# Reordered tail of the last expert, earlier merge tile, scores over two key tiles, and a modulation row split 2/6

## The reference

```python
# first block
h = rms_norm(x, norm1_g); p = h @ w_in
merged = g_a * (gmlp(...) @ w_up_a) + g_b * (s5(...) @ w_up_b)
x = x + merged @ w_out
h2 = rms_norm(x, norm2_g)
# expert choice: 16 experts, each takes its 128 best tokens
gate, idx = lax.top_k(softmax(h2 @ w_router).T, 128)
xs = h2[idx]
y = (silu(xs @ w_gate) * (xs @ w_up)) @ w_down * gate      # 1024 -> 2048 -> 1024
x = rms_norm(x + segment_sum(y, idx), final_g)
# second block
shift, scale, gate = split(silu(c) @ w_mod + b_mod)
h = rms_norm(x, g_pre) * (1 + scale) + shift
q, k, v, g_att, u, g_lru, merge = split(h @ w_in)
y_a = (dilated_attention(q, k, v) * silu(g_att)) @ w_pa     # 3 groups, 4 heads of 128
y_b = (rg_lru(conv(u)) * silu(g_lru)) @ w_pb
out = (sigmoid(merge_a) * y_a + sigmoid(merge_b) * y_b) @ w_o
return x + gate * rms_norm(out, g_post)
```

## Time and profile before

| | |
|---|---|
| Time, median of 3 | 2869.82 us (2868.81 to 2870.44) |
| The profiled execution's own time | 2869.5 us |
| Its span in the profile | 2867.7 us |
| Mean granted TensorE clock | 0.994 of full |
| TensorE busy | 2804.5 us (98%) |
| VectorE, ScalarE, GpSimd busy | 1720.3, 1308.4, 731.2 us |

### The profile page before, as it was taken

How to read it: one execution, slowest core, us unless ns; L and a number is a source line. 1 busy time by engine, 2 the same in 40 slices (tenths; PEclk the granted TensorE clock), 3 DMA queues, 4 the chain that set the end, 5 groups by cost and what they waited for, 6 DMA issues and landing times. The chain is left out here.

```text
span 2867.7 us, 34973 instructions
## 1 busy us (share of the span) xinstructions
PE 2804.5 (98%) x13294; PEld 2302.4 (80%) x13294; DVE 1720.3 (60%) x1879; ACT 1308.4 (46%) x1544; POOL 731.2 (25%) x283
## 2 busy tenths in 40 slices
PE   7999999989999999999999999999999999999999
PEld 6887888568888888888888867889988777778887
DVE  7962114888888888888888874141312514864132
ACT  4231013467777777777777753130302211343021
POOL 0002222002222233333322322313221323333330
PEclk9999999999999999999999999999999999999999
DMA  4021114599999999999999953111111411111131
GB/s 163 23 72 40 37 52 156 227 387 392 382 384 383 382 382 383 382 384 382 381 380 377 385 202 117 45 60 45 60 49 48 141 44 59 44 44 45 52 125 59
DMA packets 127075, 555.98 MB, mean 194 GB/s; under 512 B 14545, under 2 KB 22753, under 8 KB 93825
## 3 DMA queue, kind: packets, MB, share of 16 engines
q1 hardware_dynamic: 116160, 523.91, 48.1%
q0 software_dynamic: 5328, 20.07, 2.5%
q10 hardware_dynamic: 5490, 10.62, 1.0%
HBM read 521.42 MB, written 32.09 MB: 193 GB/s over the span
## 5 line engine op out<-in xcount | busy, mean ns | idle before, releaser
L2564 DVE TENSOR_TENSOR slots_lo<-buffer,slots_hi 128x2048 fp32r<-128x2048 f32 x384 | 851.4, 2285 | 102.4 <-ACT slots_hi L1849 102.4
L1849 ACT ACTIVATE slots_hi<-buffer 128x2048 fp32r<-128x2048 f32 x384 | 708.9, 1950 | 41.2 <-PE bank L1346 26.2
L1011 PE MATMUL bank<-hT_hi,ring_hi 128*128 128x512 f32 x1216 | 483.8, 398 | 9.7 <-POOL ring_lo L913 6.1
L1013 PE MATMUL bank<-hT_hi,ring_lo 128*128 128x512 f32 x1216 | 474.7, 390 | 0.0
L1012 PE MATMUL bank<-hT_lo,ring_hi 128*128 128x512 f32 x1216 | 474.3, 390 | 0.0
L970 POOL DMA_INDIRECT xacc<-buffer x15 | 276.6, 18438 | 616.4 <-ACT buffer L1915 616.4
L910 POOL CAST ring_hi<-buffer 128x1024 fp32r<-128x1024 f32 x101 | 113.1, 1119 | 848.8 <-DMA buffer<-in_wstream 819.4
L913 POOL TENSOR_TENSOR ring_lo<-buffer,ring_hi 128x1024 fp32r<-128x1024 f32 x111 | 285.0, 2571 | 51.0 <-ACT ring_hi L1579 42.9
L1011 PEld LDWEIGHTS bank<-hT_hi,ring_hi 128*128 128x128 f32 x1216 | 228.9, 188 | 61.9 <-DVE hT_lo L2671 7.1
L1013 PEld LDWEIGHTS bank<-hT_hi,ring_lo 128*128 128x128 f32 x1216 | 228.6, 188 | 48.1
L1012 PEld LDWEIGHTS bank<-hT_lo,ring_hi 128*128 128x128 f32 x1216 | 229.1, 188 | 46.0 <-issue 1.2
(11 more groups left out here) (503 smaller groups left out, 3972.3 us busy)
## 6 DMA issues: line engine op xcount, KB each, us to landing
buffer<-in_w_gate SPq DMA_DIRECT2D x128, 1024.0 KB, 7.7
buffer<-in_w_up SPq DMA_DIRECT2D x128, 1024.0 KB, 4.9
buffer<-in_w_down SPq DMA_DIRECT2D x128, 1024.0 KB, 8.2
buffer<-in_wstream SPq DMA_DIRECT2D x154, 512.0 KB, 3.5
buffer<-in_x SPq DMA_DIRECT2D x16, 512.0 KB, 7.9
od<-buffer ACTq DMA_DIRECT2D x24, 260.0 KB, 2.1
xacc<-buffer SPq DMA_DIRECT2D x8, 512.0 KB, 2.8
h2d<-buffer SPq DMA_DIRECT2D x8, 512.0 KB, 5.0
```

The lines of the kernel that those rows point to most:

```text
L1011: mm(bank, lhs[0], rhs[0], start=first, stop=False)
L1013: return mm(bank, lhs[1], rhs[0], start=False, stop=last)
L1849: fn(slots_hi[:, n_ % NH, :], slots[n_ % NS], ACT.Copy).then_inc(slot_high_ready, 1)
L2564: tt2(slots_lo[:, place_of(n_), :], slots[n_ % NS], slots_hi[:, n_ % NH, :].bitcast(F32), ALU.subtract).then_inc(slot_split, 1)
```

## The change

The text is changed in seven places:

1. Modulation row 3 has 2 of its 8 steps ahead of the index transposes instead of 4, and 6 behind them.
2. The subtraction for the first expert's slot 0 (`slots_lo`, 128x2048) goes from DVE, where it stood between the first expert's index list and the other 15, to POOL, behind the gather; DVE waits for it before it makes the next two.
3. In every expert's down projection PE takes a slot's two steps of f for half 0, then both for half 1. For the last expert a semaphore is given after half 0's last pass, and ACT takes half 0 on it.
4. `last_rows` goes (0,0), (1,0), (0,1), (1,1) in (tile, half), and PE no longer waits for both halves of `last_lo` ahead of it. DVE adds in that order.
5. Scores of a tile with two key blocks: two heads a bank over 256 keys instead of four heads a bank over 128 keys. Masks lie side by side.
6. SP issues the load of tile `I_A2` ahead of its wait for attention's stores and of the loads of the combination.
7. ACT writes `att_hi` of tiles 6 and 7 ahead of the drains of `GA` 2's halves instead of behind both.

The diff, cut to its core:

```diff
     LRU_TILES += [("lg", 2 * _q - 2 + _c) for _c in range(2) if _q > 0]
+LAST_ORDER = [(0, 0), (1, 0), (0, 1), (1, 1)] + [(tt, h) for tt in range(2, 8) for h in range(2)]
...
     for j in range(8):
-        b.add(("last", j // 2, j % 2), "dve")
+        b.add(("last",) + LAST_ORDER[j], "dve")
     for j in range(2):
...
         M0 = 42 * K
-        mask_cur = at(M0, P)
-        mask_prev = at(M0 + 128, P)
+        mask_both = at(M0, 2 * P)
+        mask_prev, mask_cur = mask_both[:, 0:P], mask_both[:, P:2 * P]
         mask_pair = at(M0 + 256, P)
...
                 sp.dma_start(xfd[tt * P:(tt + 1) * P, :], xf3[:, tt, :]).then_inc(xf_stored, 16)
-            for i in range(I_ATT + 4, I_A2):
+            for i in range(I_ATT + 4, I_A2 + 1):
                 load_tile(i)
...
                     comb_loaded[tt], 16)
-            for i in range(I_A2, I_LRU + 4):
+            for i in range(I_A2 + 1, I_LRU + 4):
                 load_tile(i)
...
             gather()
+            pool.wait_ge(slot_high_ready, 1)
+            nc.gpsimd.tensor_tensor(slots_lo[:, place_of(0), :], slots[0], slots_hi[:, 0, :].bitcast(F32),
+                                    ALU.subtract).then_inc(slot_split, 1)
             pool.sem_inc(ys_settled, 1)
...
                 mm(bank[:], ones16[0:NE, :], tables[0:NE, 4 * i:4 * i + 4, :], start=True, stop=True).then_inc(full1, 1)
-            mod_row(3, 0, 4)
+            mod_row(3, 0, 2)
             for j in range(2):
...
                 turn(bank[:, 0:NE], (gv if j else gif)[0][0:NE, :], ident[0:NE, 0:NE]).then_inc(full1, 1)
-            mod_row(3, 4, KD)
+            mod_row(3, 2, KD)
             pe.wait_ge(xs_loaded, 16)
...
                     w = slot_ready(16 + q)
-                    for s in range(2):
+                    if q % 2 == 0:
+                        pe.wait_ge(heT_ready, e * 4 + q // 2 + 1)
+                    for h, s in ((0, 0), (0, 1), (1, 0), (1, 1)):
                         f = 2 * q + s
-                        if f % 4 == 0:
-                            pe.wait_ge(heT_ready, e * 4 + f // 4 + 1)
-                        for h in range(2):
-                            cs = slice(s * DM + h * HALF, s * DM + (h + 1) * HALF)
-                            last = three_passes(psum[6 + h][:], (heT_hi[:, f, :], heT_lo[:, f, :]),
-                                                (w[0][:, cs], w[1][:, cs]), f == 0, f == 15)
+                        cs = slice(s * DM + h * HALF, s * DM + (h + 1) * HALF)
+                        last = three_passes(psum[6 + h][:], (heT_hi[:, f, :], heT_lo[:, f, :]),
+                                            (w[0][:, cs], w[1][:, cs]), f == 0, f == 15)
+                        if not another and (q, h, s) == (7, 0, 1):
+                            last.then_inc(up_full, 1)
                     last.then_inc(slot_used, 1)
...
-                for tt in range(first, end):
-                    for h in range(2):
-                        bank = b2.wait_free(pe, ("last", tt, h))
-                        pe.wait_ge(last_split, h + 1)
-                        hs = slice(h * HALF, (h + 1) * HALF)
-                        mm(bank[:], chosen15[:, tt * P:(tt + 1) * P], last_hi[:, hs], start=True, stop=False)
-                        mm(bank[:], chosen15[:, tt * P:(tt + 1) * P], last_lo[:, hs], start=False,
-                           stop=True).then_inc(full2, 1)
-            pe.wait_ge(last_split, 2)
+                for tt, h in LAST_ORDER[2 * first:2 * end]:
+                    bank = b2.wait_free(pe, ("last", tt, h))
+                    pe.wait_ge(last_split, h + 1)
+                    hs = slice(h * HALF, (h + 1) * HALF)
+                    mm(bank[:], chosen15[:, tt * P:(tt + 1) * P], last_hi[:, hs], start=True, stop=False)
+                    mm(bank[:], chosen15[:, tt * P:(tt + 1) * P], last_lo[:, hs], start=False,
+                       stop=True).then_inc(full2, 1)
             last_rows(0, 4)
...
                 def scores(tt):
-                    for w_ in range(1 + has_previous(g, tt)):
-                        bank = b2.wait_free(pe, ("S", g, tt, w_))
-                        for h in range(HEADS):
-                            last = mm(bank[:, h * P:(h + 1) * P], Qh[:, h, tt * P:(tt + 1) * P],
-                                      Kh[g][:, h, (tt - w_) * P:(tt - w_ + 1) * P], start=True, stop=True)
+                    nw = 1 + has_previous(g, tt)
+                    for w_ in range(nw):
+                        bank = b2.wait_free(pe, ("S", g, tt, w_))[:].rearrange("p (h k) -> p h k", k=nw * P)
+                        for i, h in enumerate(range(HEADS // nw * w_, HEADS // nw * (w_ + 1))):
+                            last = mm(bank[:, i, :], Qh[:, h, tt * P:(tt + 1) * P],
+                                      Kh[g][:, h, (tt - nw + 1) * P:(tt + 1) * P], start=True, stop=True)
                         last.then_inc(full2, 1)
...
                         for h in range(HEADS):
-                            last = turn(bank[:, h * P:(h + 1) * P], SM[tt % 2][:, h, w_ * P:(w_ + 1) * P], ident)
+                            last = turn(bank[:, h * P:(h + 1) * P], SM[tt % 2][:, h, (nw - 1 - w_) * P:(nw - w_) * P], ident)
                         last.then_inc(full2, 1)
...
                     nc.scalar.copy(scB, silu_c.unsqueeze(2).to_broadcast([P, KD, P])).then_inc(scB_ready, 1)
-                    act.wait_ge(slot_used, e * 24 + 24)
+                    act.wait_ge(up_full, e * 3 + 4)
                     for h in range(2):
+                        if h:
+                            act.wait_ge(slot_used, e * 24 + 24)
                         fn(last_hi[:, h * HALF:(h + 1) * HALF], psum[6 + h][:], ACT.Identity,
...
             for i, (kind, x, h) in enumerate(GATT_ORDER):
+                if kind == "GA" and x == 2:
+                    attention_high(6 + h)
                 if i == 1:
...
                         attention_high(x - 2)
-            attention_high(6)
-            attention_high(7)
             for f in (3, 4, 5):
...
-            slots_low(0, 0, 1)
             for e in range(1, NE):
...
             turned_rows_low(first_banks, 1, 2).then_inc(drained1["dve"], 1)
+            dve.wait_ge(slot_split, 1)
             slots_low(0, 1, AHEAD)
...
+            def add_half(tt, h):
+                hs = slice(h * HALF, (h + 1) * HALF)
+                bank = b2.wait_full(dve, ("last", tt, h))
+                dve.wait_ge(x_moved[tt], 64)
+                tt2(xin3[:, tt, hs], bank[:], xin3[:, tt, hs], ALU.add).then_inc(drained2["dve"], 1)
             def add_last(tt):
...
-                for h in range(2):
-                    hs = slice(h * HALF, (h + 1) * HALF)
-                    bank = b2.wait_full(dve, ("last", tt, h))
-                    dve.wait_ge(x_moved[tt], 64)
-                    tt2(xin3[:, tt, hs], bank[:], xin3[:, tt, hs], ALU.add).then_inc(drained2["dve"], 1)
+                for h in range(2 if tt > 1 else 0):
+                    add_half(tt, h)
+                if tt == 0:
+                    add_half(0, 0)
+                    add_half(1, 0)
+                if tt < 2:
+                    add_half(tt, 1)
                 b2.wait_drained(dve, ("last", tt, 1))
...
                         bank = b2.wait_full(dve, ("S", g, tt, w_))
-                        mask = mask_prev if w_ else (mask_pair if g == 2 else mask_cur)
-                        stt(SM[tt % 2][:, :, w_ * P:(w_ + 1) * P], bank[:].rearrange("p (h k) -> p h k", h=HEADS),
-                            HEAD_DIM ** -0.5, mask.unsqueeze(1).to_broadcast([P, HEADS, P]), ALU.mult,
-                            ALU.add).then_inc(drained2["dve"], 1)
+                        mask = mask_both if nw == 2 else (mask_pair if g == 2 else mask_cur)
+                        heads = HEADS // nw
+                        stt(SM[tt % 2][:, heads * w_:heads * (w_ + 1), 0:nw * P],
+                            bank[:].rearrange("p (h k) -> p h k", h=heads), HEAD_DIM ** -0.5,
+                            mask.unsqueeze(1).to_broadcast([P, heads, nw * P]), ALU.mult, ALU.add).then_inc(drained2["dve"], 1)
                     b2.wait_drained(dve, ("S", g, tt, nw - 1))
```

## The result

Five executions of the changed kernel have a median of 2855.85 us (2852.97 to 2857.6), five of the kernel before, on the same chip, 2870.44. The ratio is 0.9946, 95% interval 0.9935 to 0.9956: faster, by 14.6 us. The profiled execution took 2853.83 us, its span 2851.7 (2867.7 before), and its mean granted clock is 0.997 against 0.994. Predicted were 2854.8, with a range of 2851.5 to 2859.5.

A forecast was written before the change was run, and what follows sets the result against it. PE, busy 2804.5 us (98% of the span), was taken as the bound, leaving pauses and slow clocks to win; 6.6 + 4.3 + 3.0 + 0.4 + 0.4 = 14.7 us off 2869.5 gave 2854.8, range 2851.5 to 2859.5.

The forecast's parts named there:

- 1, `GA` 6's early load: Merge's first tile: loading it early removes PE's pause (5.08) and the slow passes behind it (1.54), 6.6 us.
- 2, `att_hi` 6 and 7: Before products A: roundings done in ACT's idle time remove the pause (2.74) and slow passes (1.61), 4.3 us.
- 3, the last expert's tail: Behind the last expert: working by halves brings the gate row 3.3 us nearer, 3.0 us net, ends 2.3 and 3.3.
- 4, in front of the first expert: Before the first expert: row steps moved at no cost, subtraction off DVE's queue; 0.4 us, ends 0 and 2.4.
- 5, scores: Attention scores of eleven two-key-block tiles: fewer, wider products win 0.4 us, ends 0 and 0.8.
- the allowance for the chain of adds, squares and norms: Last expert's tail: 0.3 us taken off the 3.3 because this chain might be late next.
- the term's own end of 2.4: Before the first expert: upper end of the 0.4 us gain, if the shorter pause kept the clock up.
- still 1.95 us before the gathered rows land at 582.27: Before the first expert: modulation row 3, ending 1.8 us later at 580.3, still finishes ahead of the gathered rows.
- 0.45 earlier: First expert: DVE's second half of xsT_lo could end at 586.5 instead of 586.96.
- the prediction's better rival: Before the first expert: the clock stays up, 2.0 us more won, 2852.8; chance 0.08.
- the gate row's price: Scores: 0.429 us per 512 columns, by which 8 records of 256 take 1.72 us, 0.07 less.
- The rivals that end slower or near no change: Merge's early load not coming early, 2861.4, chance 0.03; all experts' passes slower in the new order, 2875, chance 0.02.

The follow-up runs named there:

- e5: Kernel before, only the load of tile GA6 moved ahead of the attention rows; 2865.26 us, ratio 0.9979.
- e6: Kernel before, only the last two att_hi roundings moved ahead of the last two gate fills; 2867.36 us, ratio 0.9987.
- e7: Kernel before, only the down projection by halves and the last expert's rows in the new order; 2868.83 us, ratio 0.9992.
- e2: Kernel before, only the first slot's subtraction moved to GpSimd behind the gather; 2869.25 us, ratio 1.0001.
- e3: Kernel before, modulation row by 2 and 6 and first slot's subtraction on GpSimd, nothing else; 2869.14 us, ratio 0.9994.
- e8: Kernel before, only the scores over two key tiles at once; 2872.6 us, ratio 1.0005.
- e4: Kernel after, with the first slot's subtraction back on VectorE ahead of the gather; 2855.95 us, ratio 0.9948.
- e9: Kernel before, first slot's subtraction on VectorE behind the gathered rows' low parts, nothing on GpSimd; 2870.23 us, ratio 0.9997.
- e11: Kernel after, first passes wait for only half the low parts, modulation's last two VectorE operations moved into the last expert; 2851.95 us, ratio 0.9933.
- e12: Kernel after with the changes of e10 and e11 together; 2854.09 us, ratio 0.9938.
- e1: Kernel before, only the modulation row by 2 and 6 instead of 4 and 4; 2869.7 us, ratio 0.9995.
- e10: Kernel after, final norm's first two tiles reordered: four adds before the first multiplication, squares before weighted ones; 2854.73 us, ratio 0.9944.

## Why the prediction held, step by step

| term (its number in the prediction) | forecast | trace after | alone |
|---|---|---|---|
| 1, `GA` 6's early load | 6.6 | 6.63 | 6.62 (e5) |
| 2, `att_hi` 6 and 7 | 4.3 | 4.35 | 4.33 (e6) |
| 3, the last expert's tail | 3.0 | 2.46 | 2.39 (e7) |
| 4, in front of the first expert | 0.4 | 2.66 | to the first pass 1.83 (e2), 0.53 with the row slow (e3) |
| 5, scores | 0.4 | 0.66 | 0.61 (e8) |

**1 and 2** were right in mechanism and size. The pauses went whole, and the slow passes behind them with them. `GA` 7 came in time. From the attention's last transposes to the first `OT` the kernels without edit 6 take 30.58 to 32.48 us, as the pause (4.10 to 5.38) and the slow stretch behind it turn out; with it 24.57 or 24.58 in all six. The gain is 6.0 to 7.9 us, and a steadier stretch.

**3** was right at the gate row, 3.25 us nearer where 3.3 was forecast. The size that failed is the allowance for the chain of adds, squares and norms, 0.3; it came to 0.8. The chain did start earlier, but its multiplication L2669 stood against GpSimd's subtraction. In seven kernels (after, e3, e4, e7, e9, e11, e12) the first multiplication starts 0.17 to 1.97 us into a GpSimd subtraction, and in each it ends 1.08 us behind that subtraction's end, whatever its start: after, 1686.47 + 2.39 = 1688.86 and 1687.17 + 2.77 = 1689.94. In the four that have edits 3 and 4 and the old order of squares, the pause before the transposes follows it one to one:

| kernel | GpSimd's subtraction ends | multiplication starts, takes, ends | pause |
|---|---|---|---|
| e11 | 1686.83 | 1685.62, 2.29, 1687.91 | 0.17 |
| after | 1688.86 | 1687.17, 2.77, 1689.94 | 0.66 |
| e7 | 1693.90 | 1692.15, 2.83, 1694.98 | 0.71 |
| e4 | 1693.18 | 1691.23, 3.04, 1694.27 | 0.93 |

In each the multiplication less the pause is 2.11 or 2.12. That VectorE stands still until GpSimd has ended is the form in which the Trainium skill has it (SBUF — State Buffer, Who interferes with whom: with two SBUF inputs on VectorE and an SBUF read on GpSimd, one waits for the other's whole instruction); the trace agrees, with the numbers of this table, within the 0.15 us by which 1.08 falls short of the 1.23 that the multiplication takes alone. The prediction had this rule, and looked for its harm at the list in front of the first expert, where GpSimd's 4.53 us did no harm; the list's closing step came 0.35 us after its end. It wasn't carried to the tail.

The 3.25 also rested on the clock. The forecast took the slow stretch behind the pause for a property of the kernel. The same code ran there at full clock in e1, e8 and e9, 6.47 or 6.48 us, and against that edits 3 and 4 bring the gate row only 1.66 us nearer. With them the distance was 4.81 to 4.83 in all six kernels. What counts in the end is the distance from the last pass to the transposes: 21.68 to 21.80 us without the edits where the clock fell, 20.21 (e1), 20.26 (e8) and 21.20 (e9) where it didn't, 18.60 to 19.68 with them. So the profiled execution before flattered the edits: against e1 and e8 those of e7 win 0.8 us and not 2.4. The means of the eight and the six kernels, 21.31 and 19.26, lie 2.05 apart.

**4** is where a step failed, and the 2.66 us that came of it lie outside the term's own end of 2.4: "still 1.95 us before the gathered rows land at 582.27" and "0.45 earlier" take the landing as fixed. It wasn't. In the kernel before, the gather's issue began 0.36 us into VectorE's subtraction (575.62 + 2.28 = 577.90) and ended at 578.82, 0.92 behind its end. In all seven kernels with the subtraction on VectorE ahead of the ranks the issue takes 2.84 us, in the other seven 1.05:

| kernels | issue | index to transposes | index to first pass |
|---|---|---|---|
| subtraction ahead on VectorE: before, e1, e4 to e8 | 2.84 | 6.53 to 6.93 | 11.86 to 11.91 |
| on GpSimd: after, e2, e10 (e11 and e12, where the pass waits for less, left out) | 1.05 | 5.58, 5.57, 4.78 | 10.05, 10.03, 9.74 |
| on GpSimd, row slow: e3 | 1.05 | 6.30 | 11.33 |
| on VectorE behind: e9 | 1.05 | 5.29 | 11.58 |

So the 1.95 us of cover was 0.80 in the profile after, and VectorE's start of the low parts was 1.8 us earlier against the index, not 0.45: the queue is 2.28 shorter, the rows were there for it, and ACT's high parts took back the rest. The other 0.85 us are the clock, the prediction's better rival in part: it fell later, and the transposes and the first group ran fast. That part hangs on neither edit as far as the runs show, and is luck in the one profile: the first three groups took 4.22 (e7) to 5.29 us in kernels with neither edit, 4.44 (after, e10) and 5.20 (e3) with both, and 4.71 with edit 2 alone (e2).

Edit 1 was costed at nothing, which is right for the profiled execution: in both traces the index transposes start 0.33 us behind the VectorE row that releases them. In six other kernels with the row at 4 and 4 they start 0.46 to 1.62 us behind it, 1.36 and 1.62 in e7 and e8, where the clock was at half speed in the row; with 2 and 6 always 0.33 or 0.34. Edit 1 takes that lateness away, and pays at the other end when the row is slow (e3) or the rows land early: in e10, at full clock, PE came from the row straight to the transposes, and nothing was left of the cover. Which is worth more over many executions wasn't settled.

**5** stayed inside its ends, 0.61 to 0.66: an eleventh of it is 0.06 a tile, so the wider products cost about what the gate row's price gave, 0.07 less, and not the halfway value that was taken.

**The sum** came out near because the errors met: 2.3 us too little at the first expert and 0.3 at the scores, 0.5 too much at the tail, and an index that came 0.7 us later (it lies between 575.54 and 579.70 in the fourteen profiles, with the edits and without). The profiled executions differ by 15.7 us, the medians by 14.6, and the five executions of the changed kernel lie 4.6 apart, so that the median fell within 1.1 us of the forecast is partly luck. Terms 1 and 2, 10.9 of the 14.7 us, are shown by whole times too (e5, e6); terms 3, 4 and 5 by the traces alone. The upper bound of the forecast's terms is 2869.5 - 13.2 = 2856.3, not 2856.5, which changes nothing. The rivals that end slower or near no change did not happen; the pace of the experts' passes is unchanged: between the first expert's fourth group and the last expert's last pass lie 1092.61 us before and 1092.69 after.

## What to carry to other kernels

A distance between two engines' rows that stays the same while what lies between them moves (11.86 to 11.91 us in seven kernels, where the transposes moved by 0.4) points at a queue, and the instruction that stands in it is worth moving even where its engine looks far from busy. Before costing such a move, ask what stood still beside the instruction as well: here a transfer's issue on another engine. A pause that costs twice through the clock is worth its own length in every execution and the slow stretch only in some, so the two are kept apart in the sum. A VectorE instruction with two SBUF operands near a critical chain is best placed where GpSimd is idle (1.23 us for the multiplication there, 1.52 to 3.37 beside a subtraction already under way); moving it by a microsecond can merely exchange one GpSimd instruction for the next, as in e10.

## What the runs showed that was not expected

- A gather issued by GpSimd (indirect transfer, 128 rows) takes 1.05 us to issue without, and 2.84 beside, a 128x2048 VectorE subtraction of two SBUF operands that takes 2.28; it ends 0.92 us behind that subtraction. e9 moves nothing else and has the 1.05. Which part of the issue stands still isn't shown. The issue is 1.79 us longer; from the index to the transposes of the rows it is 6.68 us in the mean of seven kernels with it, 5.40 in six without (e3, whose transposes waited for the row, left out).
- The granted clock at one place is not the same in kernels that have the same instructions there. At the modulation row it was at half speed in e1, e3, e7 and e8, and at full speed in the ten others; behind the last expert's pause of 2.34 us it stayed up in e1, e8 and e9 and fell in the kernel before, e2, e3, e5 and e6. What decides it isn't in these traces, and stays open.
- How much of the work behind a pause runs slowly also moves: after pauses of 3.3 to 4.3 us the first expert's first three groups took from 4.22 us (e7) to 5.29 (before), with the same instructions.
